# A router between two layers: early weights, another operand order, and work handed over in halves

## The chip, the cores and the metric

The kernel runs on one core of one Trainium2 chip. The metric is the device time of one execution in microseconds (us), lower is better. One program computes two blocks of two layers each on 256 tokens with 1024 features, all in float32 or in a split form of it (below).

## What the kernel must compute

Only the second layer of the first block touches the change. After its token mixer and a layer norm, its feed-forward part is a mixture of 8 experts, 2 for each token:

```python
def moe_ffn(x, router_w, router_b, w13, w2):
    logits = (x @ router_w) + router_b                 # (256, 1024) @ (1024, 8)
    top_v, top_i = lax.top_k(logits, 2)
    wts = jax.nn.softmax(top_v, axis=-1)
    gate = einsum('bsk,bske->bse', wts, one_hot(top_i, 8))
    y = zeros_like(x)
    for e in range(8):
        y = y + gate[..., e:e + 1] * swiglu(x, w13[e], w2[e])   # 1024 -> 2 x 3584 -> 1024
    return y
```

## The kernel before

**Split products.** Every large product is made of three: a float32 operand is split into a high part rounded to `F32R` (written `_hi`) and the rest (`_lo`), and `product` issues hi*hi, hi*lo and lo*hi on TensorE (lines 618 to 620). Weights come in units of 1 MB. SP loads each unit into one of 6 slots of `raw` (`load`, line 400: a slot is free again when its unit has been split), ScalarE writes `w_hi` (`split`, line 1312), VectorE writes `w_lo` (`split`, line 1697), each in one of 3 slots that TensorE frees when it has used the unit (`unit_used`). The order in which ScalarE and VectorE split, and what they do between, is written out by hand, one program for each engine; the engines meet on semaphores.

**The passage to the experts.** The mixer of the second layer ends with a layer norm on VectorE, whose two halves TensorE transposes (line 660) and ScalarE and VectorE split into `xT_hi` and `xT_lo` (`x_parts`), in four pieces. Then, in the order of the work:

1. POOL, after the norm is done, loads the router's weights `rw_raw` and bias `rb` (lines 557, 558); VectorE splits the weights (lines 2011, 2013).
2. TensorE makes the logits, 2 tiles of 128 tokens by 8 chunks of 128 features by 3 products. The tokens are the stationary operand (128 columns), the weights the moving one (8 columns).
3. VectorE adds the bias (line 2015) and ranks the experts, one tile of 128 tokens after the other: `chosen` is 1 for the 2 best of each token.
4. TensorE counts, in 5 small matmuls (lines 978 to 982), each token's slot at each expert and the tokens of each expert. Meanwhile ScalarE and VectorE make the gates.
5. VectorE makes `slot_of`, then `extra_sb` (1 if some expert has over 128 tokens, which asks for a second pass), then `y_sum` (line 2059), loads `extra_sb` into a register and makes `pick`, the one-hot matrix that gathers the first expert's tokens (line 2067). TensorE and ScalarE wait for `extra_sb` too and load it.
6. TensorE gathers the tokens with `pick` (`dispatch`, line 991), ScalarE and VectorE split them into `xg_hi` and `xg_lo` (`tokens`, lines 1507 and 2073) in two pieces, and TensorE starts the first expert when both are there.

**The experts.** An expert has 14 steps. A step uses three units: `up` with the value half, `up` with the gate half (24 matmuls with 256 moving columns each) and `down` (12 matmuls with 512), and two transposes between. The first two units of the first expert, 0 and 1, are split before the router; unit 2 is split by ScalarE after its first `silu`, and by VectorE after `hidden` of step 0, then unit 3 and so on. From the second expert on, `dispatch` runs inside step 9 of the expert before, and `tokens` at its end; TensorE waits for both pieces before step 0. The next line says it for all experts:

```python
if j == 0:
    pe.wait_ge(S_.xg_lo_ready, item.value(plus=1))
```

## Time and profile before

| | us |
|---|---|
| median of 3 runs (2419.69 to 2421.21) | 2420.73 |
| the profiled execution | 2413.6 |
| its span in the trace | 2411.8 |

The span is what the trace shows from the first to the last instruction. TensorE (PE) is busy in 2286.6 us of the span, VectorE (DVE) in 1750.6, ScalarE (ACT) in 1322.5. A place in the trace is given by its time from the start of the span: the passage to the experts lies between 619 and 671 us, the experts go on to about 1690 us. PE is a matmul, PEld the load of its stationary operand, PEclk the share of full speed (2.4 GHz) that TensorE's clock was granted. In a timeline row the second number is the duration, x3 says that three instructions are merged in the row, and the bracket at the end is the engine's idle time before it with what ended it.

### The profile page before, as it was taken

To read this page: it belongs to the slowest core of one execution; us is meant where nothing else is said; L and a number is where in the kernel's file an instruction comes from. 1 tells how busy PE (TensorE), PEld (TensorE's weight loads), DVE (VectorE), ACT (ScalarE), POOL (GpSimd) and SP (SyncE) were. 2 spreads that over 40 slices of the span, in tenths; PEclk is the share of its full clock that TensorE was granted. 3 is DMA by queue.
4 is the path that set the end of the run, shared out by engine and by line. 5 is a ranking of instruction groups with operands and counts; after the bars stand their busy time and mean duration, and the time that the engine had idled before them with its cause. 6 is when DMAs were issued, how large, how long until landed. Compare 5 with 4: busy or idle time off the path is not lost.

```text
span 2411.8 us, 41151 instructions
## 1 busy us (share of the span) xinstructions
PE 2286.6 (95%) x16277; PEld 2139.7 (89%) x16277; DVE 1750.6 (73%) x1881; ACT 1322.5 (55%) x1253; POOL 182.3 (8%) x178
## 2 busy tenths in 40 slices
PE   7998999999699999999999999999699999898998
PEld 7998998999689999999999999999588999887997
DVE  4565545457478888888888888888677777667777
ACT  4643443554266767676776777677345444425443
POOL 1000000100000000000000000000390000750000
PEclk9998999999699999999999999999899999879999
DMA  9344655534289999999999999999433555323541
GB/s 303 106 148 133 207 177 170 172 114 159 78 301 340 350 334 349 333 351 353 334 349 332 350 334 351 335 349 341 141 105 115 175 196 175 128 88 122 198 174 56
DMA packets 423432, 556.44 MB, mean 231 GB/s; under 512 B 9746, under 2 KB 377092, under 8 KB 423344
## 3 DMA queue, kind: packets, MB, share of 16 engines
q1 hardware_dynamic: 419232, 544.85, 66.5%
q0 software_dynamic: 4112, 10.38, 1.4%
q8 instruction: 60, 0.98, 0.2%
q14 instruction: 28, 0.23, 0.0%
HBM read 554.13 MB, written 1.06 MB: 230 GB/s over the span
## 4 chain that ended last, share of the span: by engine, by line
issue 46%; PE 42%; DVE 6%; ACT 3%; DVEq 2%; DMA 1%; ACTq 0%; SPq 0%; POOL 0%; POOLq 0%
PE ps L618 12%; PE ps L619 12%; PE ps L620 12%; DVE w_lo L1697 2%; ACT w_hi L1312 2%; PE ps L1188 1%; PE ps L660 1%; DVEq L2164 1%; DVE cvT L2163 0%; PE ps L809 0%; DMA raw<-in_w_in 0%; DVE xn L1733 0%; PE ps L1186 0%; DVE x L1791 0%; PE ps L801 0%
## 5 line engine op out<-in xcount | busy, mean ns | idle before, releaser
L1697 DVE TENSOR_TENSOR w_lo<-raw,w_hi 128x2048 fp32r<-128x2048 f32 x519 | 1180.0, 2284 | 348.6 <-ACT w_hi L1312 347.1
L1312 ACT ACTIVATE w_hi<-raw 128x2048 fp32r<-128x2048 f32 x519 | 987.3, 1909 | 246.6 <-PE ps L620 236.3
L618 PE MATMUL ps<-w_hi,xg_hi 128*128 128x256 f32 x1792 | 515.0, 287 | 9.9 <-DVE xg_lo L2073 7.1
L618 PE MATMUL ps<-xT_hi,w_hi 128*128 128x256 f32 (+1 forms) x1712 | 494.2, 289 | 11.2 <-DVE xT_lo L1707 6.7
L620 PE MATMUL ps<-w_hi,xg_lo 128*128 128x256 f32 x1792 | 503.8, 281 | 0.0
L619 PE MATMUL ps<-w_lo,xg_hi 128*128 128x256 f32 x1792 | 503.3, 281 | 0.0
L619 PE MATMUL ps<-xT_lo,w_hi 128*128 128x256 f32 (+1 forms) x1712 | 489.4, 286 | 0.0
L620 PE MATMUL ps<-xT_hi,w_lo 128*128 128x256 f32 (+1 forms) x1712 | 489.0, 286 | 0.0
L618 PEld LDWEIGHTS ps<-w_hi,xg_hi 128*128 128x128 f32 x1792 | 338.4, 189 | 17.4 <-issue 11.1
L618 PEld LDWEIGHTS ps<-xT_hi,w_hi 128*128 128x128 f32 (+1 forms) x1712 | 332.7, 194 | 16.3 <-issue 8.8
L619 PEld LDWEIGHTS ps<-w_lo,xg_hi 128*128 128x128 f32 x1792 | 338.9, 189 | 4.0
L620 PEld LDWEIGHTS ps<-w_hi,xg_lo 128*128 128x128 f32 x1792 | 338.5, 189 | 0.0
L619 PEld LDWEIGHTS ps<-xT_lo,w_hi 128*128 128x128 f32 (+1 forms) x1712 | 332.4, 194 | 1.6
L620 PEld LDWEIGHTS ps<-xT_hi,w_lo 128*128 128x128 f32 (+1 forms) x1712 | 332.1, 194 | 0.4
L618 PE MATMUL ps<-w_hi,hT_hi 128*128 128x512 f32 x536 | 212.7, 397 | 1.0 <-DVE hT_lo L2083 1.0
L619 PE MATMUL ps<-w_lo,hT_hi 128*128 128x512 f32 x536 | 212.0, 396 | 0.0
L620 PE MATMUL ps<-w_hi,hT_lo 128*128 128x512 f32 x536 | 211.8, 395 | 0.0
L618 PE MATMUL ps<-w_hi,xT_hi 128*128 128x256 f32 (+1 forms) x448 | 130.9, 292 | 8.0 <-DVE w_lo L1697 4.3
L619 PE MATMUL ps<-w_lo,xT_hi 128*128 128x256 f32 (+1 forms) x448 | 128.7, 287 | 0.0
L620 PE MATMUL ps<-w_hi,xT_lo 128*128 128x256 f32 (+1 forms) x448 | 128.6, 287 | 0.0
L1511 ACT ACTIVATE sa<-ps 128x256 f32<-128x256 f32 x112 | 43.3, 387 | 148.6 <-PE ps L620 148.5
L620 PEld LDWEIGHTS ps<-w_hi,hT_lo 128*128 128x128 f32 x536 | 100.7, 188 | 24.2
(442 smaller groups left out, 2795.6 us busy)
## 6 DMA issues: line engine op xcount, KB each, us to landing
raw<-in_exp_w SPq DMA_DIRECT2D x336, 1024.0 KB, 5.6
raw<-in_ffn_w_up SPq DMA_DIRECT2D x44, 1024.0 KB, 5.0
raw<-in_w_in SPq DMA_DIRECT2D x42, 1024.0 KB, 6.9
raw<-in_ffn_w SPq DMA_DIRECT2D x33, 1024.0 KB, 4.9
raw<-in_ffn_w_down SPq DMA_DIRECT2D x22, 1024.0 KB, 5.3
raw<-in_w_gate SPq DMA_DIRECT2D x16, 1024.0 KB, 5.3
raw<-in_w_out SPq DMA_DIRECT2D x8, 1024.0 KB, 4.8
raw<-in_w_o SPq DMA_DIRECT2D x6, 1024.0 KB, 5.6
```

Source lines behind the costliest of these rows:

```text
L618: pe.matmul(out, lhs[0], rhs[0], start=first, stop=False)
L619: pe.matmul(out, lhs[0], rhs[1], start=False, stop=False)
L620: return pe.matmul(out, lhs[1], rhs[0], start=False, stop=last)
L660: m = pe.transpose(o[:, c, t, :], src[:, t, (2 * b + c) * P:(2 * b + c + 1) * P], ident)
L1188: m = pe.matmul(o, qgm[rows, h // 2, t, j, :], st8[rows, 4 * t + j, h // 2, :], start=False, stop=j == 3)
L1312: act.activation(w_hi[:, u.const % SPL, 0:width], raw[:, u.const % RAW, 0:width], ACT.Copy)\
L1511: act.activation(sa[:, odd, 0:FFC], ps[:, 6, 0:FFC], ACT.Silu).then_inc(S_.silue_ready, 1)
L1697: dve.tensor_tensor(w_lo[:, u.const % SPL, 0:width], raw[:, u.const % RAW, 0:width], w_hi[:, u.const % SPL, 0:width].bitcast(F32), ALU.sub ...
L2164: dve.drain()
```

## The change

- POOL loads the router's weights and bias in the first layer; VectorE splits them in the mixer of the second layer, ahead of its wait for `f_ln` (line 1876). Their tiles get places of their own.
- The logits are made with the weights as the stationary operand (8 columns) and the tokens moving (256 columns), so they come out transposed. ScalarE copies them (`lg8`), TensorE transposes them back in two pieces, VectorE adds the bias.
- Both tiles of tokens are ranked in one sequence of instructions. Two matmuls give the slots, and two more the totals, each with a semaphore of its own.
- VectorE makes the first `pick` as soon as the slots are there; totals and `extra_sb` follow. The gates and `y_sum` are made in `gates()`, behind `hidden` of step 0.
- Unit 2 is split by ScalarE and VectorE at the start of `router()`.
- Tokens are handed over in halves: `dispatch` signals after 4 of 8 chunks, `tokens` signals each piece, and the first `up` of each expert waits for a piece ahead of chunks 0 and 4.

```diff
@@ -252,6 +252,10 @@
             w_if = sb("w_if", [P, 12, FROW + 4], scope=b1)
             b_if = sb("b_if", [FROW + 4, 1], scope=b1)
             sel = sb("sel", [FROW + 4, HM], scope=b1)
+            rw_raw = sb("rw_raw", [P, KC, E_N], scope=b1)
+            rb = sb("rb", [P, E_N], scope=b1)
+            rw_hi = sb("rw_hi", [P, KC, E_N], F32R, scope=b1)
+            rw_lo = sb("rw_lo", [P, KC, E_N], F32R, scope=b1)
             with ExitStack() as m1:
                 with ExitStack() as s:
@@ -311,12 +315,9 @@
                 eo_hi = sb("eo_hi", [P, D], F32R, scope=s)
                 eo_lo = sb("eo_lo", [P, D], F32R, scope=s)
                 y_sum = sb("y_sum", [P, TT, D], scope=s)
-                rw_raw = sb("rw_raw", [P, KC, E_N], scope=s)
-                rw_hi = sb("rw_hi", [P, KC, E_N], F32R, scope=s)
-                rw_lo = sb("rw_lo", [P, KC, E_N], F32R, scope=s)
-                rb = sb("rb", [P, E_N], scope=s)
+                lg8 = sb("lg8", [E_N, S], scope=s)
                 lg = sb("lg", [P, TT, E_N], scope=s)
-                cmp2 = sb("cmp2", [P, 2, E_N, E_N], scope=s)
+                cmp2 = sb("cmp2", [P, 2, TT, E_N * E_N], scope=s)
                 rt = sb("rt", [P, 6, TT, E_N], scope=s)
         with ExitStack() as b2:
             cst2 = const_tile("cst2", CONST2, b2)
@@ -553,7 +554,7 @@
                 pool.sem_inc(S_.pool_passed, 1)
                 pool.dma_start(norm_gb[:, 0, :], over(A["ln_g"][L, 1], D)).then_inc(S_.norm_loaded, 16)
                 pool.dma_start(norm_gb[:, 1, :], over(A["ln_b"][L, 1], D)).then_inc(S_.norm_loaded, 16)
-                if L:
+                if L == 0:
                     pool.dma_start(rw_raw[:], A["router_w"][0].rearrange("(k p) e -> p k e", p=P)).then_inc(S_.router_loaded, 16)
                     pool.dma_start(rb[:], over(A["router_b"][0], E_N)).then_inc(S_.router_loaded, 16)
@@ -964,22 +965,24 @@
             def router():
-                pe.wait_ge(S_.rw_split, 1)
+                for k in range(KC):
+                    if k % 2 == 0:
+                        pe.wait_ge(S_.xT_lo_ready, 12 + (9 + k // 2))
+                    m = product(ps[0:E_N, 4, 0:S], [v[:, k, :] for v in (rw_hi, rw_lo)], [v[:, k, :] for v in (xT_hi, xT_lo)],
+                                k == 0, k == KC - 1)
+                m.then_inc(S_.logits_psum, 1)
+                pe.wait_ge(S_.lg8_ready, 1)
                 for t in range(TT):
-                    for k in range(KC):
-                        if t == 0 and k % 2 == 0:
...
-                m.then_inc(S_.logits_psum, 1)
+                    m = pe.transpose(ps[:, 6, E_N * t:E_N * (t + 1)], lg8[:, t * P:(t + 1) * P], ident[0:E_N, 0:E_N])
+                m.then_inc(S_.lgT_psum, 1)
                 pe.wait_ge(S_.chosen_ready, 1)
                 chosen = rt[:, 1]
-                pe.matmul(ps[:, 5, 0:8], K["before"], chosen[:, 0], start=True, stop=True)
-                pe.matmul(ps[:, 5, 8:16], K["before"], chosen[:, 1], start=True, stop=False)
-                pe.matmul(ps[:, 5, 8:16], ones, chosen[:, 0], start=False, stop=True)
-                pe.matmul(ps[:, 5, 16:24], ones, chosen[:, 0], start=True, stop=False)
-                pe.matmul(ps[:, 5, 16:24], ones, chosen[:, 1], start=False, stop=True).then_inc(S_.slots_psum, 1)
+                pe.matmul(ps[:, 5, 0:16], K["before"], chosen.rearrange("p t e -> p (t e)"), start=True, stop=False)
+                pe.matmul(ps[:, 5, 8:16], ones, chosen[:, 0], start=False, stop=True).then_inc(S_.slots_psum, 1)
+                for t in range(TT):
+                    m = pe.matmul(ps[:, 7, 0:8], ones, chosen[:, t], start=t == 0, stop=t == TT - 1)
+                m.then_inc(S_.totals_psum, 1)
             def experts(extra):
@@ -990,11 +993,14 @@
                         for t in range(TT):
                             m = pe.matmul(bank(0, KC, P)[:, k, :], x[:, t, k * P:(k + 1) * P], pick[:, t, :],
                                           start=t == 0, stop=t == TT - 1)
-                    m.then_inc(S_.xg_psum, 1)
-                def up(at, half):
+                        if k % 4 == 3:
+                            m.then_inc(S_.xg_psum, 1)
+                def up(at, half, tokens=None):
                     w = unit_parts(at, KC, FFC)
                     for k in range(KC):
+                        if tokens is not None and k % 4 == 0:
+                            pe.wait_ge(S_.xg_lo_ready, tokens.value(2, 1 + k // 4))
                         m = product(ps[:, (6, 2)[half], 0:FFC], [v[:, k, :] for v in (xg_hi, xg_lo)],
                                     [v[:, k, :] for v in w], k == 0, k == KC - 1)
                     m.then_inc(S_.unit_used, 1)
@@ -1017,10 +1023,8 @@
                 def step(item, j):
                     n, at = moe_step(item, j)
-                    if j == 0:
-                        pe.wait_ge(S_.xg_lo_ready, item.value(plus=1))
                     pe.wait_ge(S_.silue_ready, n.value(plus=1))
-                    up(at, 0)
+                    up(at, 0, item if j == 0 else None)
                     hidden_T(n + -1)
                     up(at + 1, 1)
                     if j == 1:
@@ -1079,9 +1083,8 @@
                     plain_steps(item, DISPATCH_STEP + 1)
                 dispatch(Count(0))
-                pe.wait_ge(S_.xg_lo_ready, 1)
                 pe.wait_ge(S_.silue_ready, 1)
-                up(Count(MOE_UNIT0), 0)
+                up(Count(MOE_UNIT0), 0, Count(0))
                 up(Count(MOE_UNIT0 + 1), 1)
                 for j in range(1, EARLY):
                     step(Count(0), j)
@@ -1496,14 +1499,17 @@
                 square_root(S_.sqrt_in, S_.sqrt_out, count, stat[:, 120:122])
             def router():
+                split(Count(MOE_UNIT0 + 2))
+                act.wait_ge(S_.logits_psum, 1)
+                act.activation(lg8[:], ps[0:E_N, 4, 0:S], ACT.Copy).then_inc(S_.lg8_ready, 1)
                 act.wait_ge(S_.rexp_in, 1)
                 act.activation(rt[:, 0], rt[:, 0], ACT.Exp).then_inc(S_.rexp_out, 1)
             def experts(extra):
                 def tokens(item):
-                    act.wait_ge(S_.xg_psum, item.value(plus=1))
                     for b in range(2):
+                        act.wait_ge(S_.xg_psum, item.value(2, b + 1))
                         act.activation(xg_hi[:, 4 * b:4 * b + 4, :], bank(b, 4, P), ACT.Copy).then_inc(S_.xg_hi_ready, 1)
                 def silu(at, odd):
@@ -1546,7 +1552,6 @@
                 act.activation(stat[:, 7:8], ones[:, 0:1], ACT.Copy).then_inc(S_.put_ready, 1)
                 tokens(Count(0))
                 silu(Count(MOE_UNIT0), 0)
-                split(Count(MOE_UNIT0 + 2))
                 for j in range(1, EARLY):
                     step(Count(0), j, False)
                 with act.Fori(0, extra * E_N + (E_N - 1)) as e:
@@ -1872,6 +1877,11 @@
                 split(u + 6)
                 split(u + 7)
                 split(u + 8)
+                if L:
+                    dve.wait_ge(S_.router_loaded, 32)
+                    dve.tensor_copy(rw_hi[:], rw_raw[:])
+                    dve.drain()
+                    dve.tensor_tensor(rw_lo[:], rw_raw[:], rw_hi[:].bitcast(F32), ALU.subtract)
                 dve.wait_ge(S_.f_ln, L + 1)
                 dve.scalar_tensor_tensor(rowe[:], rowx[0:HM, :], 0.0, rowe[:], ALU.min, ALU.subtract)
@@ -2007,55 +2017,58 @@
                 x_parts(L * 12 + 8, 0)
             def router():
-                dve.wait_ge(S_.router_loaded, 32)
-                dve.tensor_copy(rw_hi[:], rw_raw[:])
...
-                    dve.tensor_copy(gate_of[:, :, b * E_N:(b + 1) * E_N], rt[:, 0])
+                split(Count(MOE_UNIT0 + 2))
+                dve.wait_ge(S_.lgT_psum, 1)
+                dve.tensor_tensor(lg[:], bank(6, TT, E_N), spread(rb[:], 1, TT), ALU.add)
+                dve.drain()
+                other, own = spread(lg[:], 2, E_N), spread(lg[:], 3, E_N)
+                pairs = [cmp2[:, i].rearrange("p t (e j) -> p t e j", e=E_N) for i in range(2)]
+                dve.tensor_tensor(pairs[0], other, own, ALU.is_gt)
+                dve.tensor_tensor(pairs[1], other, own, ALU.is_equal)
+                dve.reduce_max(col(100, 2), lg[:], AX_X)
+                dve.drain()
+                dve.tensor_tensor(cmp2[:, 1], cmp2[:, 1], spread(K["lower"], 1, TT), ALU.mult)
+                dve.tensor_tensor(rt[:, 0], lg[:], spread(col(100, 2), 2, E_N), ALU.subtract).then_inc(S_.rexp_in, 1)
+                dve.drain()
+                dve.tensor_tensor(cmp2[:, 0], cmp2[:, 0], cmp2[:, 1], ALU.add)
+                dve.drain()
+                dve.reduce_sum(rt[:, 2], pairs[0], AX_X)
+                dve.drain()
+                dve.tensor_scalar(rt[:, 1], rt[:, 2], 2.0, None, ALU.is_lt).then_inc(S_.chosen_ready, 1)
+                dve.drain()
+                dve.tensor_scalar(rt[:, 4], rt[:, 1], 4.0 * S, -4.0 * S, ALU.mult, ALU.add)
                 dve.wait_ge(S_.slots_psum, 1)
                 dve.tensor_tensor(rt[:, 3], rt[:, 1], bank(5, TT, E_N), ALU.mult)
-                dve.tensor_scalar(rt[:, 4], rt[:, 1], 4.0 * S, -4.0 * S, ALU.mult, ALU.add)
-                dve.reduce_max(col(102), ps[:, 5, 16:24], AX_X)
                 dve.drain()
                 dve.tensor_tensor(slot_of[:, :, 0:E_N], rt[:, 3], rt[:, 4], ALU.add)
+                dve.drain()
+                for t in range(TT):
+                    m = dve.tensor_scalar(pick[:, t, :], K["iota"], slot_of[:, t, 0:1], None, ALU.is_equal)
+                m.then_inc(S_.pick_ready, 1)
+                dve.wait_ge(S_.totals_psum, 1)
+                dve.reduce_max(col(102), ps[:, 7, 0:8], AX_X)
+                dve.drain()
                 dve.tensor_scalar(extra_sb[:], stat[0:1, 102:103], float(P), 1.0, ALU.is_gt, ALU.mult).then_inc(S_.extra_ready, 1)
-                dve.drain()
                 dve.tensor_scalar(slot_of[:, :, E_N:2 * E_N], slot_of[:, :, 0:E_N], float(P), None, ALU.subtract)
                 dve.memset(slot_of[:, :, 2 * E_N:], -1.0)
                 dve.memset(gate_of[:, :, 2 * E_N:], 0.0)
+                dve.drain()
+            def gates():
+                dve.wait_ge(S_.rexp_out, 1)
+                dve.tensor_tensor(rt[:, 0], rt[:, 0], rt[:, 1], ALU.mult)
+                dve.drain()
+                dve.reduce_sum(col(100, 2), rt[:, 0], AX_X)
+                dve.drain()
+                dve.reciprocal(col(100, 2), col(100, 2))
+                dve.drain()
+                dve.tensor_tensor(rt[:, 0], rt[:, 0], spread(col(100, 2), 2, E_N), ALU.mult)
+                dve.drain()
+                for b in range(2):
+                    dve.tensor_copy(gate_of[:, :, b * E_N:(b + 1) * E_N], rt[:, 0])
                 dve.tensor_scalar(y_sum[:], x[:], ALPHA, None, ALU.mult).then_inc(S_.y_added, 1)
                 dve.drain()
@@ -2070,9 +2083,8 @@
                 def tokens(item):
                     for b in range(2):
                         dve.wait_ge(S_.xg_hi_ready, item.value(2, b + 1))
-                        m = dve.tensor_tensor(xg_lo[:, 4 * b:4 * b + 4, :], bank(b, 4, P),
-                                              xg_hi[:, 4 * b:4 * b + 4, :].bitcast(F32), ALU.subtract)
-                    m.then_inc(S_.xg_lo_ready, 1)
+                        dve.tensor_tensor(xg_lo[:, 4 * b:4 * b + 4, :], bank(b, 4, P), xg_hi[:, 4 * b:4 * b + 4, :].bitcast(F32),
+                                          ALU.subtract).then_inc(S_.xg_lo_ready, 1)
                 def hidden(at, odd):
                     used(at + 1)
@@ -2114,11 +2126,10 @@
                         tokens_of(item + 1)
                 dve.memset(stat[:, 6:7], 0.0).then_inc(S_.eo_lo_ready, 1)
-                tokens_of(Count(0))
                 tokens(Count(0))
                 dve.wait_ge(S_.silue_ready, 2)
                 hidden(Count(MOE_UNIT0), 0)
-                split(Count(MOE_UNIT0 + 2))
+                gates()
                 for j in range(1, EARLY):
                     step(Count(0), j, False)
                 with dve.Fori(0, extra * E_N + (E_N - 1)) as e:
```

## Rows read from the trace of the kernel before

**Rows 1.** Waits of TensorE in the whole kernel: waiter <- awaited: total us, times, longest.

```profile
PE ps L618 <- DVE xg_lo L2073: 7.1, 8, 2.0
```

**Rows 2.** Windows: busy us (instructions) of PE, PEld, DVE, ACT, POOL; PEclk, DMA share, GB/s.

```profile
634.80:645.20 10.40, 10.40 (x48) 10.31 (x48) 0.00 (x0) 0.00 (x0) 0.00 (x0) 0.50 0.00 0
654.30:662.30 8.00, 5.48 (x32) 5.29 (x32) 1.78 (x5) 1.93 (x3) 0.00 (x0) 0.75 0.00 0
672.20:675.20 3.00, 3.00 (x16) 3.00 (x15) 3.00 (x2) 0.00 (x0) 0.00 (x0) 0.50 1.02 341
710.00:750.00 40.00, 40.00 (x288) 37.50 (x287) 34.50 (x25) 29.29 (x25) 0.00 (x0) 1.00 1.05 360
```

**Rows 3.** Timeline, TensorE, then VectorE, ahead of the logits (start, us, engine, line).

```profile
627.42 1.94 PE L660 MATMUL ps<-cst,x 128*128 128x128 f32 x8 [0.88 <-DVE x L1752]
634.80 0.38 PE L618 MATMUL ps<-rw_hi,xT_hi 128*128 128x8 f32 x1 [5.43 <-DVE rw_lo L2013]
...
630.03 0.69 DVE L1707 TENSOR_TENSOR xT_lo<-ps,xT_hi 128x512 fp32r<-128x512 f32 x1 [0.16 <-ACT xT_hi L1327]
634.25 0.20 DVE L2011 CAST rw_hi<-rw_raw 128x64 fp32r<-128x64 f32 x1 [3.52 <-DMA rb<-in_router_b]
```

**Rows 4.** Timeline, TensorE, then ScalarE, second block: a product with 16 stationary columns.

```profile
1731.40 0.28 PE L619 MATMUL ps<-xT_lo,w_hi 128*16 128x256 f32 x1
...
1733.94 0.28 PE L620 MATMUL ps<-xT_hi,w_lo 128*16 128x256 f32 x1
...
1734.25 0.38 ACT L1583 ACTIVATE gT<-ps 16x256 f32<-16x256 f32 x1 [2.12 <-PE ps L620]
```

**Rows 5.** Timeline, VectorE: from the logits to the chosen experts.

```profile
645.24 0.17 DVE L2015 TENSOR_TENSOR lg<-ps,rb 128x16 f32<-128x16 f32 x1 [10.50 <-PE ps L620]
...
648.74 0.06 DVE L2033 MEMSET stat<- 128x1 f32 x1
```

**Rows 6.** Timeline, VectorE, then ScalarE: from the slots to the first pick.

```profile
651.22 0.17 DVE L2048 TENSOR_TENSOR rt<-rt,ps 128x16 f32<-128x16 f32 x1 [0.90 <-PE ps L982]
...
651.71 0.13 DVE L2054 TENSOR_SCALAR extra_sb<-stat 1x1 int32<-1x1 f32 x1
...
652.04 1.22 DVE L2059 TENSOR_SCALAR y_sum<-x 128x2048 f32<-128x2048 f32 x1
...
654.30 0.48 DVE L2067 TENSOR_SCALAR pick<-cst,slot_of 128x128 f32<-128x128 f32 x2
...
652.67 0.20 ACT L1545 ACTIVATE stat<-cst 128x1 f32<-128x1 f32 x1 [3.63 <-DVE extra_sb L2054]
```

**Rows 7.** Timeline, TensorE and ScalarE: gathering and splitting the first expert's tokens.

```profile
654.84 5.48 PE L991 MATMUL ps<-pick,x 128*128 128x128 f32 x32 [3.66 <-DVE pick L2067]
662.33 0.39 PE L618 MATMUL ps<-w_hi,xg_hi 128*128 128x256 f32 x1 [2.01 <-DVE xg_lo L2073]
...
660.36 1.09 ACT L1507 ACTIVATE xg_hi<-ps 128x512 fp32r<-128x512 f32 x2 [7.38 <-PE ps L991]
```

**Rows 8.** Timeline, VectorE, then TensorE: the first expert's second and third unit.

```profile
668.34 0.42 DVE L2079 TENSOR_TENSOR hf<-sa,ps 128x256 f32<-128x256 f32 x1 [6.07 <-PE ps L620]
668.68 6.69 DVE L1697 TENSOR_TENSOR w_lo<-raw,w_hi 128x2048 fp32r<-128x2048 f32 x3
...
671.11 0.36 PE L618 MATMUL ps<-w_hi,xg_hi 128*128 128x256 f32 x1 [2.88 <-DVE w_lo L1697]
...
675.69 0.36 PE L618 MATMUL ps<-w_hi,xg_hi 128*128 128x256 f32 x1
```

**Rows 9.** Timeline, VectorE, then TensorE: the second expert's tokens.

```profile
789.07 1.28 DVE L2073 TENSOR_TENSOR xg_lo<-ps,xg_hi 128x512 fp32r<-128x512 f32 x2
...
790.59 0.38 PE L618 MATMUL ps<-w_hi,xg_hi 128*128 128x256 f32 x1 [0.73 <-DVE xg_lo L2073]
```

**Rows 10.** Timeline, VectorE in the second layer's mixer, at the wait for f_ln.

```profile
479.62 0.41 DVE L1877 SCALAR_TENSOR_TENSOR rowe<-rowx,rowe 4x256 f32<-4x256 f32 x1 [5.10 <-ACT rowe L1418]
```

**Rows 11.** DMA issues: count, KB each, median us from issue to landing.

```profile
raw<-in_exp_w SPq DMA_DIRECT2D x336, 1024.0 KB, 5.6
```

36 lines of the change are left out of this document (7 added, 29 removed).

## The prediction, made before the change was run

> **What bounds the kernel now.** I read the busy shares first, then the waits of TensorE, then windows and timelines of the passage from the second mixer to the experts. Once the experts run, TensorE is the bound: from 710 to 750 us it is busy 40.00 of 40.00 us at the full clock, with VectorE at 34.50 and ScalarE at 29.29 [rows 2]. A weight unit lands 5.6 us after its issue [rows 11] and there are six slots; with 62 matmuls in a step of three units (288 in 40.0 us, so 8.6 us), the ring turns once in 17 us, so transfers do not set the pace. What is taken off the passage therefore moves everything behind it by as much, and what is taken off a wait of TensorE at each expert's start counts 7 times more [rows 1].
>
> The passage is one chain: last transposes of the norm from 627.42, logits from 634.80 [rows 3], the bias add at 645.24, chosen experts at 648.74 [rows 5], slots at 651.22, pick at 654.30 [rows 6], gathering from 654.84, first expert from 662.33 [rows 7], a hole of 2.88 us before its third unit at 671.11, and its fourth at 675.69 [rows 8]. I work out where each of these comes in the changed kernel, in the clock of the old trace.
>
> **Logits.** Their first wait is for the bias transfer: VectorE sat 3.52 us until 634.25, while the last `xT_lo` was ready at 630.03 + 0.69 = 630.72 [rows 3]. With the weights loaded a layer earlier TensorE starts behind its transposes, 8 passes from 627.42 at 0.21 us: at 629.1. The four pieces of `xT_lo` stay ahead of it (it needs the last at about 633.0). The 48 old matmuls took 10.40 us at half clock [rows 2], 0.217 us each. The new form is 24 matmuls with 256 moving columns. A product of this form with 16 stationary columns stands in the second block: 22 matmuls in 2.54 us, 0.115 us each, at full clock [rows 4], so the small weight load is hidden. At 1.2 GHz 256 columns are 0.213 us: 24 x 0.213 = 5.1 us, to 634.2, and 0.3 us until the result is there, as in the old end. If the clock rose in the middle, it would be 1.5 us less; if the weight loads were not hidden, I bound them by the whole old cost of a matmul, 24 x 0.217 = 5.2 us more, which the form in rows 4 makes unlikely.
>
> One rule of the Trainium skill speaks against this edit. The page TensorE: Matmul & The Clock Gate, section LDWEIGHTS, puts a load at its columns over 1.2 GHz, 107 ns for 128. By it the old 48 matmuls would be an estimated 5.1 us, the same as the new ones, and the exchange of operands would be worth nothing. The trace has twice that, 0.217 us each [rows 2], and the row decides: the exchange is worth 5 us.
>
> **Back to tokens in rows.** New is ScalarE's copy, 0.38 us as the nearest row has it [rows 4], and two transposes, four passes with 128 stationary columns: 3 x 0.21 + 0.35 = 1.0 us. The bias add comes at 634.5 + 0.4 + 1.0 = 635.9, against 645.24. Bounds for the round trip: 0.8 us (full clock) and 2.0 (twice the transposes).
>
> ScalarE and VectorE split unit 2 in the meantime. ScalarE is free at 630.0 and done at 631.9, VectorE ends at 634.3 (2.29 us a split, a third of 6.69 [rows 8]). Both lie under the logits; only if these ended before 632.9 would the split be the later one, and then by under 1.4 us.
>
> **Ranking.** From add to chosen it was 3.50 us [rows 5], two tiles of 1.6 us and 0.25 for the add. One sequence over both tiles is one tile's 1.6 plus four operations wider by 64 elements (0.07 each) plus the wider maximum: 2.2 us. Chosen at 638.1, saving 1.3.
>
> **Slots and the first pick.** Five small matmuls stood between 648.80 and 651.22, 2.4 us or 0.43 for each plus the way out [rows 5, 6]; two are left: 1.1 us, slots at 639.2. Then product, sum and two picks, with their drains about 1.0 us: pick ready at 640.2. But TensorE cannot gather yet: it still waits for `extra_sb` and its register. Two more matmuls give the totals at 640.0, VectorE takes them behind the picks, maximum, drain and `extra_sb` 0.4 us: 640.5. ScalarE needed 0.83 us from `extra_sb` to its next operation (651.71 + 0.13 to 652.67) [rows 6]. For TensorE the old trace shows only that it took under 3.0 us (651.84 to 654.84), since it was hidden behind the pick. I take 1.0, nearest to ScalarE's row, and keep 0.8 and 3.0. Gathering starts at 641.5, against 654.84: 13.3 us saved. The gates never set the end here: VectorE was idle 0.90 us for the slots behind them [rows 6].
>
> **Gathering and the first two units.** Old: 7.49 us from 654.84 to 662.33 [rows 7], 5.48 of them busy, at a mean clock of 0.75 [rows 2], so about 16 of 32 passes at 0.213 and the rest at 0.117. In halves, the first 4 chunks are signalled after 3.6 us, ScalarE takes 0.6 (1.09 for two [rows 7]), VectorE 0.7 (1.28 for two [rows 9]) and TensorE 0.24 (790.35 to 790.59 [rows 9]): 5.2 us, just as the gathering ends at 5.4. The second half is ready at 7.1, the first four chunks of `up` last until 6.8, then comes a wait of 0.3. `up` on unit 0 ends 8.5 us after the start instead of 10.4: 1.9 us saved, at 650.0. Unit 1 follows to 652.9 and unit 2, now split, to 655.8; the hole of 2.88 us [rows 8] is gone.
>
> **What is late next.** `gates()` and `y_sum` now stand in VectorE's queue between `hidden` and the split of unit 3. `hidden` starts at 653.1, its successor at 653.45; the gates' operations are 1.2 us (they filled the time before the slots), `y_sum` 1.22 [rows 6], a split 2.29: unit 3 is there at 658.3, TensorE asks for it at 655.9. A new hole of 2.5 us, against the old `up` on unit 3 at 675.69 [rows 8]: 658.4, **17.3 us earlier**. Behind unit 3, VectorE's splits of 4 and 5 end at 660.5 and 663.0 and are wanted at 661.3 and 664.1, so no further hole.
>
> **The clock.** The old hole of 2.88 us was followed by half clock: 0.50 from 672.20 to 675.20 [rows 2]. That cost, 3.4 us at half pace or 1.5 us of work, lies before 675.69 and is in the 17.3 as saved. The new hole is 2.5 us, nearer to the one of 2.88 after which the clock fell than to the one of 2.01 [rows 7] after which it held. I take it that it falls: **minus 1.5 us**. The gathering's clock is taken as before; had it risen earlier or later it would be worth up to 1.5 us either way.
>
> **Each further expert.** TensorE waited 7.1 us in 8 waits for `xg_lo`, 2.0 of them at the first [rows 1], so 0.73 at each of 7 others. At the second, VectorE's two pieces ran from 789.07 to 790.35 and TensorE began at 790.59 [rows 9]. With the first piece enough it begins 0.6 us earlier, and the second piece is there before chunk 4 (1.4 us later). 7 x 0.6 = **4.2 us**, at most 5.1, at least 0.
>
> **Edits at nothing.** VectorE's split of the router's weights (about 0.5 us) goes in front of a wait in which it is idle 5.10 us [rows 10]; were that gone, it would cost 0.5. The two loads on POOL in the first layer come last before a long wait of that queue, and nobody needs them before 474 us, where VectorE's idle time of rows 10 begins; they might delay one weight unit by the 3.5 us that VectorE waited for them, which six slots hide. The moved `exp` reads a result that nobody wants until 653; its table load now stands behind ScalarE's copy, off the chain.
>
> **Sum.** 17.3 - 1.5 + 4.2 = 20.0 us. Against the profiled execution's own 2413.6 that is 2393.6. The median shown is 7.1 us above that execution; I take the same difference, and 2420.7 - 20.0 = **2400.7**.
>
> **Rivals.**
>
> - *The clock is kinder*: it holds over the 2.5 us hole, or rises within the logits. For it: the gap is shorter than the old one, and TensorE now works from 627.4 to 634.2 with hardly a pause. Against: half clock through 10.4 us of old logits [rows 2]. 21.5 to 23.0 us, so 2397.7 to 2399.2. Chance 0.22.
> - *TensorE's own start is late*: its register turn costs near 3.0 instead of 1.0 us, or gathering starts just so that it runs all through at half clock (1.5 us more). For it: nothing in the old trace bounds it better. 16 to 18 us, 2402.7 to 2404.7. Chance 0.14.
> - *The early handover does nothing*: at experts 2 to 8 the units or VectorE's splits, not `xg_lo`, end the wait, and TensorE waits later in the step for what it gained. For it: VectorE splits two units on end there. Against: TensorE is busy without a gap in the steps [rows 2]. 15.8 us, 2404.9. Chance 0.07.
> - *Slower*: the choppier work leaves TensorE at half clock into the experts. A step of 8.6 us costs 8.6 x (0.213/0.117 - 1) = 7.1 us more at 1.2 GHz, so three steps in a row at half clock eat the 20 us; from four on the kernel is slower, at four 2429. Against it: the old gathering, begun at half clock, had a mean of 0.75, and the experts run at 1.00 from 710 us on [rows 2]. Chance 0.02; 0.03 that it ends near no change in this way.
>
> My forecast has 0.5, its own range being 2398.5 to 2403. The rest, 0.02, is anything else. Range for 8 in 10: 2396.5 (kind clock and 5.1 at the experts) to 2406 (late start or no handover gain, some of both). A measurement of this kernel can tell about 0.2%, 4.8 us, from no change. Faster by more than that 0.94, within it 0.04, slower 0.02.
>
> **What would show it.** Logits of about 5 us starting near 629, at PEclk 0.5; bias add 9 us earlier; the gathering waiting for `extra_sb`, not for the pick; no wait between gathering and first `up` beyond 0.3 us, none at unit 2, 2 to 2.6 us at unit 3; waits for `xg_lo` of about 0.1 us in each later expert. Wrong would be: matmuls of 0.4 us in the logits, a gathering that starts after 643, or a step cadence other than 8.6 us.

## The result, and the profile after

The changed kernel took 2389.47 us, the median of 4 runs (2383.73 to 2396.32). The kernel before took 2420.21 us (4 runs, 2411.11 to 2421.21: the three of the table above, and 2411.11). The ratio is 0.9889, with a 95% interval of 0.9869 to 0.9908. The forecast of 2400.7 us had the direction right and was 11.2 us too slow. The time also lies 7.0 us under the low end of the range, 2396.5.

One thing has to be seen first. The two profiled executions differ by 2413.6 - 2396.32 = 17.3 us, the two medians by 30.7. The first is less than the 20.0 that I worked out, the second is more. So there are two questions: did the parts of the change save what the sum says, and where does the rest of the difference lie?

**The passage.** Timeline of TensorE in the changed kernel (start, us, engine, line). These rows answer to [rows 3, 7 and 8].

```profile
627.34 1.94 PE L661 MATMUL ps<-cst,x 128*128 128x128 f32 x8 [0.87 <-DVE x L1757]
628.93 0.56 PE L619 MATMUL ps<-xT_hi,rw_hi 128*8 128x256 f32 x1
...
632.61 0.28 PE L621 MATMUL ps<-xT_hi,rw_lo 128*8 128x256 f32 x1
633.35 0.29 PE L976 MATMUL ps<-cst,lg 8*128 8x8 f32 x2 [0.46 <-ACT lg L1504]
636.27 0.39 PE L981 MATMUL ps<-rt,cst 128*128 128x16 f32 x2 [2.63 <-DVE rt L2038]
...
639.09 6.44 PE L994 MATMUL ps<-pick,x 128*128 128x128 f32 x32 [1.76 <-DVE extra_sb L2054]
...
656.73 0.38 PE L619 MATMUL ps<-w_hi,xg_hi 128*128 128x256 f32 x1 [2.17 <-DVE w_lo L1702]
```

The gathering starts at 639.09 and its releaser is `extra_sb`, as foretold. Timeline of VectorE over the same stretch, which answers to [rows 5, 6, 8]:

```profile
631.75 2.29 DVE L1702 TENSOR_TENSOR w_lo<-raw,w_hi 128x2048 fp32r<-128x2048 f32 x1 [1.11 <-ACT w_hi L1315]
633.95 0.17 DVE L2022 TENSOR_TENSOR lg<-ps,rb 128x16 f32<-128x16 f32 x1
...
637.42 0.48 DVE L2048 TENSOR_SCALAR pick<-cst,slot_of 128x128 f32<-128x128 f32 x2
...
638.06 0.14 DVE L2054 TENSOR_SCALAR extra_sb<-stat 1x1 int32<-1x1 f32 x1
...
643.53 0.69 DVE L2086 TENSOR_TENSOR xg_lo<-ps,xg_hi 128x512 fp32r<-128x512 f32 x1 [4.16 <-ACT xg_hi L1513]
646.20 0.69 DVE L2086 TENSOR_TENSOR xg_lo<-ps,xg_hi 128x512 fp32r<-128x512 f32 x1 [1.98 <-ACT xg_hi L1513]
...
653.06 1.22 DVE L2072 TENSOR_SCALAR y_sum<-x 128x2048 f32<-128x2048 f32 x1
654.38 4.49 DVE L1702 TENSOR_TENSOR w_lo<-raw,w_hi 128x2048 fp32r<-128x2048 f32 x2
```

The bias add follows the split of unit 2 without a pause, at 633.95: the logits were done early enough for the split to be the later one, the case that the prediction set apart. The gates and `y_sum` stand ahead of unit 3's split, and behind it comes the new hole in TensorE, 2.17 us. Windows of the changed kernel (busy us and instructions of PE, PEld, DVE, ACT, POOL; then PEclk, DMA share, GB/s), against [rows 2]:

```profile
628.90:632.70 3.80, 3.80 (x26) 2.54 (x24) 2.34 (x3) 2.56 (x3) 0.00 (x0) 0.73 0.84 267
639.00:647.00 8.00, 7.91 (x45) 7.73 (x45) 1.44 (x3) 2.30 (x5) 0.00 (x0) 0.65 0.00 0
658.20:661.70 3.50, 3.50 (x17) 3.31 (x17) 3.50 (x4) 0.61 (x1) 0.00 (x0) 0.51 1.05 363
1760.70:1788.00 27.30, 26.64 (x106) 22.62 (x107) 11.04 (x32) 2.98 (x8) 24.30 (x23) 0.50 0.14 46
```

In the logits the clock rose midway (mean 0.73), in the gathering it was low in all but the last us, and behind the hole at unit 3 it fell. The fourth line lies in the second block. There TensorE has 27.30 us at 1.2 GHz, while it is busy 26.64 us of them. In the trace of the kernel before that the prediction rests on, this place has 10.2 us of half clock. This is one of the places where this execution loses part of what the passage gained.

Waits of TensorE and its weight loads in the whole changed kernel (us, times, longest), against [rows 1]:

```profile
PEld ps L619 <- DVE xg_lo L2086: 2.9, 8, 0.4
```

The matmuls no longer wait for `xg_lo`. Only the loads still do, 8 times, 0.4 us at most.

**A landmark.** To separate the parts I measure each trace from the first transpose ahead of the logits (L661, before L660) to the start of VectorE's last `eo_lo`, near the end of the last expert. I call this time the landmark. Its rows, from the timelines of the kernel before and then of the changed kernel:

```profile
624.61 1.94 PE L660 MATMUL ps<-cst,x 128*128 128x128 f32 x8 [5.44 <-DVE x L1752]
...
1691.58 1.22 DVE L2089 TENSOR_TENSOR eo_lo<-ps,eo_hi 128x1024 fp32r<-128x1024 f32 x1 [0.61 <-ACT eo_hi L1520]
```

```profile
624.53 1.94 PE L661 MATMUL ps<-cst,x 128*128 128x128 f32 x8 [5.44 <-DVE x L1757]
...
1669.88 1.23 DVE L2101 TENSOR_TENSOR eo_lo<-ps,eo_hi 128x1024 fp32r<-128x1024 f32 x1 [0.62 <-ACT eo_hi L1526]
```

Before it was 1691.58 - 624.61 = 1067.0 us, in the changed kernel 1669.88 - 624.53 = 1045.4: the change saved 21.6 us up to there. What is behind that point is nearly all the second block, the same code in both kernels. It took 2411.8 - 1691.6 = 720.2 us before and 2394.5 - 1669.9 = 724.6 in the changed kernel, so this execution lost 4.4 us there.

### The profile page after: what moved, and what is told of

The parts are those of the page before. It is cut to its first block, busy times and chain, and to the rows that moved or that the text cites. A ratio compares the mean times of both kernels' runs of the same rounds, so it can differ in the third digit from the quotient of the medians.

```text
span 2394.5 us, 41114 instructions
## 1 busy us (share of the span) xinstructions
PE 2283.5 (95%) x16253; PEld 2135.1 (89%) x16253; DVE 1746.6 (73%) x1872; ACT 1322.0 (55%) x1254; POOL 181.6 (8%) x178
## 4 chain that ended last, share of the span: by engine, by line
issue 45%; PE 42%; DVE 7%; ACT 3%; DVEq 2%; DMA 1%; ACTq 0%; SPq 0%; POOL 0%; POOLq 0%
PE ps L619 12%; PE ps L620 12%; PE ps L621 12%; DVE w_lo L1702 2%; ACT w_hi L1315 2%; PE ps L1191 1%; PE ps L661 1%; DVE cvT L2174 0%; PE ps L1189 0%; DVEq L2175 0%; PE ps L810 0%; DMA raw<-in_w_in 0%; DVE xn L1738 0%; DVE x L1796 0%; PE ps L802 0%
```

## The experiments

**The changed kernel again, and both kernels with TensorE kept at work.** The first run repeats the changed kernel. The other two add 26 dummy products (their results are not read) ahead of a wait of TensorE in each of the second block's two mixers, in the kernel before and in the changed one:

```diff
                 T(7)
+                for i in range(26):
+                    pe.matmul(ps[:, 2, 0:S], xT_hi[:, i % 8, 0:P], xT_hi[:, (i + 1) % 8, :], start=True, stop=True)
                 pe.wait_ge(S_.state_ready, L + 1)
```

> The changed kernel once more, beside the kernel before. Theory A (the passage and the experts' handovers save 21.7 us up to the last expert's eo_lo, as in the two traces, and the rest of the measured difference is where TensorE's clock happens to be low in the second block): the trace shows the saving up to the end of the experts between 20 and 23.5 us again, while the differences of whole executions scatter by 10 us or more, mean 22 to 28. Theory B (the change speeds up something in the second block too): the second block is shorter than before in every trace by the same 4 to 6 us.

> The kernel before, with 26 matmuls of 256 columns into an unused bank put where TensorE waits 3.5 us for state_ready in both mixers of the second block. Theory A: the clock stays at 2.4 GHz through gla_out and the scores; the kernel is 4 to 14 us faster than before (it lost 10 us of clock there in the trace of before and 27 us in that of after, at 1.2 GHz), and its executions scatter less. Theory B: no more than 2 us of change, the added matmuls only fill the wait.

> The changed kernel with the same 26 matmuls in both mixers of the second block. Theory A: against the fed kernel before it is faster by 22 us, give or take 3, since the clock's lottery there is gone from both. Theory B: it is faster by 26 us or more. Against the kernel before: 28 to 36 us.

The changed kernel gave 2389.08 us again (6 runs; ratio 0.988, 0.9862 to 0.9897), and its landmark 1667.27 - 623.37 = 1043.9 us. In this trace the clock did not fall behind the hole at unit 3, which is the 1.5 us between 1045.4 and 1043.9. The stretch behind the landmark took 723.1 us, no less than the 720.2 before, so Theory B is out. With the dummies the kernel before took 2398.9 us (5 runs; 0.9916, 0.9904 to 0.9929), the changed one 2376.69 (5 runs; 0.9829, 0.9816 to 0.9843). Between them lie 22.2 us, where between the kernels as they are lay 30.7 in the first comparison and 2418.37 - 2389.08 = 29.3 in this one. The dummies alone are worth 19.5 us to the kernel before, more than the 4 to 14 expected, and 12.4 to the changed one. Windows from the landmark to the end, first the kernel before with dummies, then the changed one; the last line is one of the two places behind the dummies, in the changed kernel:

```profile
1692.20:2399.00 706.80, 647.29 (x4522) 600.31 (x4522) 525.58 (x807) 312.44 (x326) 163.22 (x140) 0.95 0.42 141
```

```profile
1669.00:2374.90 705.90, 646.65 (x4522) 600.00 (x4522) 524.93 (x807) 311.97 (x326) 162.73 (x140) 0.95 0.42 141
1759.20:1786.50 27.30, 27.30 (x215) 25.15 (x215) 19.41 (x40) 10.24 (x18) 26.27 (x22) 1.00 0.14 42
```

That place ran at full clock where the changed kernel had 0.50, and behind the landmark the two kernels now take 706.8 and 705.9 us, nearly the same. So the change's own work gives 22 us. That the rest of the difference between the medians is half clock in the second block, of which the kernel before lost more in those runs, fits this but is not seen in a trace.

**The gates ahead of the tokens.** On VectorE `gates()` goes from behind `hidden` to ahead of the first `tokens`, where it waits for the gathering anyway.

```diff
+                gates()
                 tokens(Count(0))
                 dve.wait_ge(S_.silue_ready, 2)
                 hidden(Count(MOE_UNIT0), 0)
-                gates()
```

> The changed kernel with gates() and y_sum in front of VectorE's first tokens() (it was idle for 4.16 us there) and no longer behind hidden of step 0. Theory A: the hole of 2.17 us at unit 3 goes, and with it the stretch of 3.4 us at half clock behind it (1.5 us of work): the end of the experts comes 3.5 us earlier, at 1667.5 or so for eo_lo where it was 1669.9. A rival: another wait takes its place (the split of unit 4, or hidden itself), and the end comes less than 1 us earlier.

The hole at unit 3 is gone, and the landmark is 1663.33 - 621.96 = 1041.4 us, 2.5 to 4 us less. The median was 2388.43 us (4 runs; 0.9877, 0.9861 to 0.9892), which can't be told from the changed kernel. Behind the landmark this execution took 721.9 us, five more than the late split and the late register below (717.0 and 717.1).

**One piece again; the old operand order.** The next two each undo one part of the change: the handover in halves, and the logits with the tokens moving. These two and the late split of unit 2 below ran once each, for their traces (2396.13, 2393.16 and 2389.10 us; the kernel before beside them 2412.46). One execution says nothing of a median here, so only their landmarks are used.

```diff
-                        if k % 4 == 3:
-                            m.then_inc(S_.xg_psum, 1)
+                    m.then_inc(S_.xg_psum, 2)
...
-                        if tokens is not None and k % 4 == 0:
-                            pe.wait_ge(S_.xg_lo_ready, tokens.value(2, 1 + k // 4))
+                        if tokens is not None and k == 0:
+                            pe.wait_ge(S_.xg_lo_ready, tokens.value(2, 2))
```

> The changed kernel with the tokens handed over in one piece again: TensorE adds its two counts behind the last of the eight gathering products, and `up` waits for both pieces ahead of its first product. Measured from the first transpose of the router's weights to the last w_lo-side result of the last token expert (eo_lo), the changed kernel took 1045.4 and 1043.9 us in its two traces. Theory A (the halves save 0.6 us at each of the seven later experts, 4.2 together, and 1.9 at the first): 1050 to 1052 us. Rival (the early half does nothing, since the second half's wait ends where the one wait ended): 1044 to 1045.5 us.

The landmark is 1677.68 - 624.64 = 1053.0 us, 7.7 more than in the changed kernel's first trace. Its `up` on unit 3 begins 35.8 us after the first transpose instead of 32.2, so the first expert has 3.6 of it and the seven others together 4.1. The seven agree with the 4.2 of the sum. The first expert's share is twice what Theory A had, and a window of this run says why: behind its wait for the tokens (2.10 us) the clock fell once more, in the middle of the first `up`.

```profile
648.20:651.40 3.20, 3.20 (x17) 3.20 (x16) 0.00 (x0) 0.00 (x0) 0.00 (x0) 0.50 0.00 0
```

I estimate that at 1.4 us (15 products at 0.213 us instead of 0.119), which leaves 2.2 us for the early start of the first expert, near the 1.9 of the sum.

```diff
-                    m = product(ps[0:E_N, 4, 0:S], [v[:, k, :] for v in (rw_hi, rw_lo)], [v[:, k, :] for v in (xT_hi, xT_lo)], ...)
+                        m = product(ps[:, 6, 8 * t:8 * t + 8], [v[:, k, t * P:(t + 1) * P] for v in (xT_hi, xT_lo)],
+                                    [v[:, k, :] for v in (rw_hi, rw_lo)], k == 0, k == KC - 1)
```

> The changed kernel with the logits in the old operand order (tokens stationary, router weights moving, no copy and no transposes back), weights still loaded and split early. Same stretch as in the run beside it (changed kernel 1045.4 and 1043.9 us). The logits of the old order took 10.40 us at the half clock; the new order's logits took 3.68 us, with 1.34 us more for the copy and the transposes back up to the bias add. Theory A (operand order matters): if the clock stays low, 10.4 + 0.1 - 5.0 = 5.5 us longer, 1049.5 to 1051; if the clock rises in the middle, as it did in the changed kernel, some 2 us longer, 1046 to 1047.5. Rival (the gain of the logits was the early weights alone, and the new order gives back what it saves): 1044 to 1045.5.

Timeline and window of the old operand order (TensorE):

```profile
628.99 0.35 PE L619 MATMUL ps<-rw_hi,xT_hi 128*128 128x8 f32 x1
629.20 0.35 PE L620 MATMUL ps<-rw_lo,xT_hi 128*128 128x8 f32 x1
```

```profile
629.00:639.20 10.20, 10.20 (x50) 10.20 (x48) 3.68 (x3) 3.80 (x4) 0.00 (x0) 0.50 0.60 206
```

The 48 small products take 10.2 us and stay at half clock, 0.213 us each, with the loads busy all the time (PEld 10.20). The landmark is 1674.73 - 624.58 = 1050.2 us, 4.8 more than in the changed kernel's first trace, inside the range that Theory A gave for a low clock. Part of it is the clock: in the new form it rose within the logits, here it did not. The start, 4.4 us behind the first transposes against 10.2 before, comes from the early weights alone and stays.

**Unit 2 split late; the register loaded late.** Both change the version with the gates early. The first puts the split of unit 2 back behind the first expert's hidden values on both engines. The second lets TensorE fetch its register behind the gathering.

```diff
             def router():
-                split(Count(MOE_UNIT0 + 2))
...
+                split(Count(MOE_UNIT0 + 2))      # behind silu (ScalarE) and behind hidden (VectorE)
```

> The kernel with the gates ahead of the tokens (1041.4 us in the same stretch), and the split of unit 2 put back to its old place, behind the first expert's hidden values on both engines. Theory A (the early split of unit 2 removes a wait of TensorE ahead of unit 2, and unit 3's split comes behind it on the same engines): about 2.5 to 3.5 us longer, 1044 to 1045. Rival (VectorE and ScalarE have the time anyway; the early split only moved work, and makes the ranking start later): 1040.5 to 1041.5.

The old hole of 2.88 us at unit 2 comes back, as this row of TensorE's timeline shows, and the clock falls behind it (half clock from 654.8 for 3.4 us):

```profile
654.14 0.36 PE L619 MATMUL ps<-w_hi,xg_hi 128*128 128x256 f32 x1 [2.88 <-DVE w_lo L1702]
```

The landmark is 1670.30 - 624.46 = 1045.8 us, 4.5 more than 1041.4: 2.9 for the hole and 1.6 left for the clock behind it.

```diff
                 dispatch(Count(0))
+                pe.wait_ge(S_.extra_ready, 1)
+                extra = pe.value_load(extra_sb[0:1, 0:1], min_val=0, max_val=1)
...
-                    pe.wait_ge(S_.extra_ready, 1)
-                    experts(pe.value_load(extra_sb[0:1, 0:1], min_val=0, max_val=1))
+                    experts(None)
```

> The kernel with the gates ahead of the tokens, and TensorE no longer loads the register `extra` ahead of the first gathering but behind it. In the changed kernel TensorE waits 1.76 us for extra_sb (0.9 us of it is the register load's own turn). Theory A (the passage is a chain: what is taken out of it comes off whole): the gathering starts 1.5 to 2 us earlier after the ranking, and the stretch from the first transpose of the router's weights to the last token expert's eo_lo shrinks from 1041.4 to 1039.5 to 1040 us. Rival (the tokens' copies then wait for the late register, or the load behind the gathering costs TensorE the same 0.9 us ahead of unit 0): 1040.5 to 1041.5. Whole kernel: 1 to 2 us under the 2388.4 of the version without it, if the second block's clock stays as it is; that clock alone can move it by 10 us.

Two rows of TensorE's timeline, the first with the register early (gates early), the second, in its own fence, with the register late:

```profile
636.53 6.46 PE L994 MATMUL ps<-pick,x 128*128 128x128 f32 x32 [1.76 <-DVE extra_sb L2054]
```

```profile
636.74 5.47 PE L994 MATMUL ps<-pick,x 128*128 128x128 f32 x32 [0.63 <-DVE pick L2049]
```

TensorE now waits for the pick, 0.63 us instead of 1.76, and the gathering itself is 1.0 us shorter, because the half clock around it lasts 3.4 us instead of 6.8. The landmark is 1662.60 - 623.32 = 1039.3 us, 2.1 less, of which 1.0 is thus the clock's. The median was 2382.49 us (4 runs; 0.9867, 0.9843 to 0.9891).

**TensorE kept warm in the router.** To the last version come 20 dummy products ahead of the wait for the ranking and 4 behind the totals. The run after it has the 26 of the second block too.

```diff
                 m.then_inc(S_.lgT_psum, 1)
+                for i in range(20):
+                    pe.matmul(ps[:, 3, 0:S], xT_hi[:, i % 8, 0:P], xT_hi[:, (i + 1) % 8, :], start=True, stop=True)
                 pe.wait_ge(S_.chosen_ready, 1)
```

> The version beside it with TensorE kept at work while it waits in the router: 20 dummy products of 256 columns ahead of the wait for the ranking, 4 more behind the totals, into a bank that nobody reads. Theory A: the clock, which fell 5 us behind the logits and held the first gathering at half speed (6.44 us for 64 products), stays up; the gathering takes 3.3 to 4 us, and the stretch to the last eo_lo shrinks by 2 to 3.5 us, to 1036.5 to 1038 us. Rival (the tokens' copies and the expert's first units bound it, not the gathering): less than 1 us.

> The version beside it with the 26 dummy products in the second block's mixers as well, which gave 12.4 us on the changed kernel. Theory A: 2376.7 - 5.5 (gates early, register late) - 2.5 (gathering at full clock), so 2368 to 2373 us; faster than both kernels. Rival (what the router's passage gives is lost to the clock later on, as in the run with the gates early): 2375 to 2378 us.

Timeline of TensorE with the router kept warm, then two rows of VectorE:

```profile
633.71 2.65 PE L979 MATMUL ps<-xT_hi 128*128 128x256 f32 x20
...
637.99 3.84 PE L998 MATMUL ps<-pick,x 128*128 128x128 f32 x32
642.64 0.36 PE L619 MATMUL ps<-w_hi,xg_hi 128*128 128x256 f32 x1 [0.81 <-DVE xg_lo L2091]
...
640.49 1.22 DVE L2077 TENSOR_SCALAR y_sum<-x 128x2048 f32<-128x2048 f32 x1
641.80 1.39 DVE L2091 TENSOR_TENSOR xg_lo<-ps,xg_hi 128x512 fp32r<-128x512 f32 x2
```

The gathering ran at full clock, 3.84 us instead of 5.47. Yet the landmark fell only from 1039.3 to 1038.3, by 0.9 us, so the rival was right: `y_sum` now ends at 641.71, behind ScalarE's first half (640.08 + 0.60), and VectorE's first half waits for it, so TensorE waits 0.81 us for `xg_lo`. A faster engine ran into the work that had been put into its old wait. The medians are 2379.31 us (4 runs; 0.9853, 0.9828 to 0.9877) and, with the second block's dummies, 2367.24 (5 runs, 2364.18 to 2376.58; 0.9803, 0.9778 to 0.9827). The latter is the fastest version of this study, 22 us under the changed kernel.

**Where the second block starts.** The kernel before once more, then with its last `eo_lo` computed once or twice too often; the same two in the changed kernel; and the changed kernel once more.

```diff
                 split(at + 1)
+                dve.wait_ge(S_.eo_hi_ready, item.value(plus=1))
+                for i in range(1):     # or 2
+                    dve.tensor_tensor(eo_lo[:], bank(4, D), eo_hi[:].bitcast(F32), ALU.subtract)
+                    dve.drain()
                 expert_out(item)
```

> The kernel before, unchanged, for more traces and times of it. The trace on which the prediction rests took 2413.6 us; most other runs of the kernel took 2418 to 2421. The question is where these 6 us lie. Theory A (the second block's clock): up to the last eo_lo the trace agrees with the first one within 1 us (1691.6; 1067.0 from the first transpose of the router's weights), and a run near 2420 has its extra time behind that, as more time at the half clock. Rival: the time lies in the experts or ahead of them, so that the prediction read a first block that was too short.

> The kernel before with its last eo_lo on VectorE computed one time more, which starts the second block 1.3 us later against everything ahead of it (one row of 1.23 us and a drain). Theory C (where the second block starts against the clock's switches decides how much of it runs at half speed, and the change moved that by luck): the median moves by something else than 1.3 us, by up to 8 us either way. Rival D (the second block's share is the same wherever it starts): 1.3 us slower, 2420 to 2421.

> The same with the last eo_lo computed two times more, a delay of 2.6 us. Theory C: the median moves by something else than 2.6 us, and otherwise than with one. Rival D: 2.6 us slower, 2421 to 2423.

> The changed kernel with its last eo_lo computed one time more (1.3 us). Theory C: the median leaves 2389 by something else than 1.3 us, up to 8 us either way. Rival D: 1.3 us slower, 2390 to 2391.

> The changed kernel with its last eo_lo computed two times more (2.6 us). With one repeat its median went from 2389 to 2394. Theory C (the second block's time depends on where it starts against the clock's switches): other than 2.6 us slower; since one repeat of 1.3 us cost 5 us here, and a repeat in the kernel before gave 4 us back and the second took 12, no size is foretold, only that it lies off the straight line by 3 us or more. Rival D: on the line, 2391 to 2392.

> The changed kernel once more, for its spread: its ten runs so far lie from 2383.7 to 2396.3, those of the kernel before in two groups, 2411 to 2414 and 2418 to 2421. Theory: the mean difference over all runs is that of the landmarks (21.7 us) plus what the second block's clock takes more from the kernel before, 3 to 8 us; so 25 to 29 us between the means.

| kernel | runs | median us | ratio to before (95%) | landmark | from the landmark's end to the kernel's |
|---|---|---|---|---|---|
| before again | 10 | 2413.8 | 0.9999 (0.9985 to 1.0013) | 1066.8 | 720.3 |
| before, +1.3 us | 10 | 2409.11 | 0.9973 (0.996 to 0.9985) | 1068.3 | 714.5 |
| before, +2.6 us | 10 | 2421.53 | 1.0022 (1.0011 to 1.0033) | 1069.7 | 727.4 |
| changed again | 5 | 2385.21 | 0.9873 (0.9849 to 0.9897) | 1044.0 | 715.8 |
| changed, +1.3 us | 4 | 2394.06 | 0.9903 (0.988 to 0.9926) | 1045.3 | 725.0 |
| changed, +2.6 us | 4 | 2398.55 | 0.9924 (0.9906 to 0.9941) | 1046.6 | 726.8 |

Adding 1.3 us of useless work made the kernel before 4.7 us faster, and adding 2.6 made it 7.7 slower than it was in the same session; by the means it is 7.0 faster and 6.7 slower (2408.2 and 2421.9 against 2415.2 over 35 runs). Rival D, under which the delay costs what it is, is out for the kernel before. In the changed kernel 1.3 us cost 5 to 9 us and 2.6 us cost 9 to 13, by which of its medians one takes. There the four runs with 1.3 us (2391.1 to 2395.6) lie within the spread of the kernel itself (15 runs, 2377.7 to 2396.3) and settle nothing; the four with 2.6 us (2398.5 to 2399.1) lie above all of it. The landmarks moved as they should, by 1.3 to 2.9 us, so the rest lies behind them. Windows from the end of the last `eo_lo` to the end of the kernel, before with one repeat, then with two:

```profile
1692.60:2405.80 713.20, 649.80 (x4470) 600.72 (x4470) 522.91 (x806) 309.91 (x325) 159.95 (x140) 0.94 0.41 139
```

```profile
1695.40:2421.70 726.30, 663.41 (x4470) 612.51 (x4470) 521.14 (x807) 309.38 (x324) 159.84 (x140) 0.92 0.41 136
```

Both have 4470 matmuls. The second is 13.1 us longer, TensorE is busy 13.6 us more with them, and the mean granted clock is 0.92 instead of 0.94. VectorE and ScalarE did the same work in nearly the same time. In these rows nothing but the clock accounts for the 13 us.

The same two places of the second block, one in each mixer, in three executions: the trace of the kernel before that the prediction rests on, its second trace, and the run with two repeats.

```profile
1781.50:1808.50 27.00, 25.57 (x165) 22.70 (x166) 16.32 (x42) 6.45 (x15) 25.80 (x23) 0.81 0.17 55
2129.70:2153.40 23.70, 23.70 (x97) 20.14 (x97) 10.42 (x29) 3.00 (x8) 16.25 (x15) 0.50 0.14 45
```

```profile
1781.30:1808.30 27.00, 25.93 (x103) 21.91 (x104) 10.39 (x32) 2.99 (x8) 24.77 (x23) 0.50 0.16 52
2132.90:2156.60 23.70, 21.78 (x134) 18.96 (x135) 13.88 (x39) 2.98 (x8) 19.96 (x18) 0.79 0.22 72
```

```profile
1784.90:1811.90 27.00, 26.18 (x104) 22.17 (x105) 10.75 (x32) 2.98 (x8) 24.46 (x23) 0.50 0.15 49
2139.90:2163.60 23.70, 23.70 (x98) 20.36 (x99) 10.38 (x30) 2.99 (x8) 16.36 (x14) 0.50 0.14 45
```

Each trace of the kernel itself has one of the two places at half clock throughout, and both take 720 us behind the landmark. The run with two repeats has both places so, and takes 727.4.

The changed kernel itself has two executions that part at such a place. The first two fences are of its second trace, the other two of the last one. Each pair has TensorE's wait for `st` in the last mixer (timeline) and the window behind it:

```profile
2106.98 0.49 PE L1189 MATMUL ps<-vc,atT 128*128 128x128 f32 x2 [3.53 <-DVE st L2266]
```

```profile
2108.10:2132.00 23.90, 23.90 (x98) 20.11 (x97) 8.99 (x27) 2.98 (x8) 20.22 (x18) 0.50 0.14 45
```

```profile
2107.29 0.49 PE L1189 MATMUL ps<-vc,atT 128*128 128x128 f32 x2 [3.52 <-DVE st L2266]
```

```profile
2108.40:2132.30 23.90, 23.90 (x163) 21.24 (x161) 14.87 (x37) 6.35 (x14) 20.48 (x18) 0.86 0.14 45
```

It is the same wait, 3.53 and 3.52 us, at nearly the same place. Behind the one the clock stays at 1.2 GHz for 23.9 us, with TensorE busy in all of them, behind the other it is low for 6.8. The first gets 98 matmuls done in this time, the second 163. The stretches behind the landmark were 723.1 and 715.8 us. The length of the wait does not decide it either: in the kernel before, the wait for `st` in the last mixer was 2.07 us ahead of the 23.7 us at half clock of its first trace, 5.13 us in its second, where the clock was low for only 10.2 us, and 1.85 us with two repeats, where it was low for 23.7 again.

## Why the prediction was right in direction and too small

**The passage** was worked out as 17.3 us up to `up` on unit 3, and it saved 675.69 - 656.73 = 19.0. Step by step:

- Logits from 629.1: they began at 628.93. Their length was 4.0 us to the copy and not 5.4, since the clock rose in the middle, in every trace of the new form. The prediction had that as a possible 1.5 us, and as a rival ("the clock is kinder", 0.22), and did not take it. The run with the old order measured 0.213 us for each product at half clock, and 4.8 us for the exchange. Here the prediction was right against the page TensorE: Matmul & The Clock Gate of the Trainium skill, section LDWEIGHTS: by 107 ns for a load of 128 columns, the estimate was that the old order costs the same as the new one.
- Bias add 633.95 instead of 635.9: 1.6 from the logits' end, and 0.7 from the transposes back (0.29 us altogether instead of 1.0), of which the split of unit 2 took 0.3.
- Ranking and slots together 3.0 us, from 633.95 to 636.92 (2.2 + 1.1 foretold), and from there to the end of `extra_sb` at 638.20 another 1.3, as foretold. TensorE's register turn was 639.09 - 638.20 = 0.9 us, 1.0 foretold between bounds of 0.8 and 3.0. Gathering 639.09 instead of 641.5.
- The gathering took 6.44 us and not 5.48. The clock, which had risen in the logits, fell again after 2.63 us of waiting for the ranking and was at 0.50 from about 637.9 to 644.6, so that half clock held for 5.5 of the 6.44 us; in the old gathering it rose in the middle. That is 1.0 back. The sum had it at nothing ("taken as before"), with up to 1.5 us either way, and as one half of the rival of the late start (0.14).
- The hole at unit 3 was 2.17 us for 2.5, with the cause as foretold: with the gates early it vanished.

**The clock behind the hole**, minus 1.5: it fell in the profiled execution. It did not in the five other traces with the same code up to there. So the term came true in one trace of six. The landmark is 1045.4 with the fall and 1043.9 to 1044.0 in three of those without. My comparison of 2.5 us with 2.88 and 2.01 rested on one example each.

**The seven handovers**, 4.2: 1013.2 us from unit 3's `up` to the last `eo_lo`, 1015.9 before; with the 1.5 of the clock that is 4.2. One piece again cost 4.1. This term was right.

**The step that failed** is the sentence "What is taken off the passage therefore moves everything behind it by as much", with the one that turned the sum into a median: "The median shown is 7.1 us above that execution; I take the same difference." The first is true up to the last expert. It is not true of the second block, which runs the same instructions in 714.5 to 727.4 us (no dummies in its mixers), and in which a shift of its start by 1.3 us alone took some 6 us off and one by 2.6 us put 7 on. The second took an offset for fixed that is a draw, and the range had room for neither. In 69 runs the kernel before has 33 between 2410.9 and 2414.1 us and 36 between 2417.4 and 2421.2. The trace that I read was of the first group, the median of three was of the second. The changed kernel has 15 runs from 2377.7 to 2396.3.

Over all these runs the means are 2416.2 and 2388.5 us, 27.7 apart. Of these, the landmark has 1067.0 - 1044.3 = 22.7 (means over three and four traces, those with the second block's dummies included). In the same traces another 0.5 lies ahead of it, which no run explains, and about 4.5 are left for the second block. The last step to the measured 30.7 is the draw: the kernel before's median lay 4.0 above its mean, the changed one's 1.0 above. So of the 10.7 us that I missed, 2.7 were sizes of terms, over half of them TensorE's clock in the first block, and some 8 were the second block and the draw. The direction was earned by the terms up to the last expert; by how much the second block added to them was luck.

What stays open: none of the traces of the kernel before is of its group near 2420. That its extra 6 to 7 us lie in the second block is inferred and not seen: the run with two repeats, which has both places at half clock, took 727.4 us there, 7.1 more than the traces of the lower group. The 4.5 us are a remainder, too: in the traces the changed kernel is not shorter there (724.6, 723.1 and 715.8 us, against 720.2 and 720.3). Nor did any run show why the same wait is once followed by a long stretch at half clock and once not; the waits agree within 0.01 us.

## What to carry to other kernels

If a sum is made from one profiled execution and told as a median, look first how the runs spread. Where they fall into groups, the offset between the trace and the median is a draw, and the range needs it, in both kernels. Here what was saved early went through unchanged only as far as TensorE ran without long waits; behind waits of 2 to 5 us the clock gave back or took several us, whatever the change was. To measure such a change, take a landmark ahead of that place, or keep TensorE at work through the wait, which was worth more here (12 us of the changed kernel) than any of the three parts of the change that a run undid.

Work put into an engine's wait is free only until that wait is shortened: in the versions with the gates early, `y_sum` held nothing up ahead of the tokens until the gathering ran at full clock, and then 0.7 of the 1.6 us that the clock gave was lost.
